# Hybrid attention and Mamba-2 step: last group split at column 272, work around it and at the start reordered

## The chip, the cores and the metric

The kernel runs on one core of one Trainium2 chip. The metric is the device time of one execution in microseconds; of several runs the median is taken. The core has five engines that this text names PE (matmuls), DVE (vector), ACT (activations), POOL (GpSimd) and SP (which only issues DMAs here).

## The reference, cut to what matters

Two layers are computed for 528 prompt tokens (16 meta tokens and 512 of the prompt) and 32 sample tokens, 560 columns in all. Layer 0 is windowed attention with sinks, layer 1 a Mamba-2 mixer. Everything is float32.

```python
hp = rmsnorm(xp, norm_w[i]); hs = rmsnorm(xs, norm_w[i])
# layer 0
q, k, v, g = split(u @ w_in); q, k = rmsnorm(q), rmsnorm(k)
out = (attend_with_sink(q, k, v) * silu(g)) @ w_out
# layer 1
z, xbc, dt = split(u @ w_in)
xs, B, C = split(silu(conv(xbc) + conv_b))
y = ssd_chunked(xs, dt, A, B, C, state) + d_skip * xs
y = y * silu(z)
y = y * rsqrt(mean over the group of y*y) * norm_w     # 4 groups of 512 channels
out = y @ w_out
xp = xp + out
```

## The kernel before, in words

Channels lie on the 128 partitions and tokens along the columns: `x` is 8 tiles of 128 x 560. Columns 0 to 15 are the meta tokens, then come four blocks of 128 prompt tokens (they begin at 16, 144, 272, 400) and from 528 on the 32 sample tokens. A float32 product is made of three fast matmuls: each operand is split into a rounded high part and a low remainder, and high x high, high x low and low x high are added (L1091 to L1093 in `project`).

**Weights.** `plan` lists the slabs (1 MB each: `kv`, `q`, `gate`, `out` of the attention stages, `dt`, `bc`, `x`, `z`, `out` of the Mamba stages) and the order of the half tiles that PE projects. SP loads a slab into one of two raw buffers, ACT rounds it (L644, `split_hi`), POOL subtracts to get the low half (L580, `split_lo`) into one of two buffers. POOL waits there until the slab two before has been used. A slab is loaded when the raw buffer is free of both.

**Order.** The order on each engine is written out by hand; a semaphore count for each product (`p_done`) and each evacuation (`p_evac`) ties them together. PE may start a half tile once the one two before has been evacuated (two PSUM banks).

**Start.** SP loads the prompt in four parts, then slabs. ACT issues the identity, meta tokens, sample tokens and six small parameter loads. PE transposes the parameters (L1141, L1142), then `x` tile by tile (L1154); ACT copies each tile out (L699) and squares rows for the norm (L693); DVE splits each tile into high and low (L1543, L1544, `split_x`). `first_tile` multiplies the first key tile as the splits appear, sums the squares (L1105) and adds the low weights (L1133).

**Between the layers.** `out` of the last attention stage is projected in 16 half tiles, and behind each finished tile DVE adds it into `x` (L1562) and splits it for layer 1 (L1543, L1544); ACT squares it (L670), POOL and DVE add up the squares, PE sums them (`sum_x`, L1113) after the `dt` projection.

**Mamba groups.** For each group g of 4, six units are run (`ORDER`: the samples, the meta block, the four prompt blocks). `start_states` on PE treats the 8 sample states in four pairs and fills with `z` half tiles (`fill_pairs`); DVE updates the states (L2023). Then for unit u: `prepare` and `new_state`, `mix` (L1862), `z` evacuation (L2007), `add_skip` of the unit before (L1896 to L1899) on DVE; `part_a`, `part_b` and a `z` half tile on PE; the decays (L971, L973) on ACT; the decay differences (L618) and the state's decay (L593) on POOL. After the last unit: SiLU of `z` (L1018), `gate_y` (L1907), squares (L1022), `sum_y` (L1408), scale (L1028, L1029), `norm_y` (L1914), high part (L927), `low_y` (L1922), each for two parts of the columns, 16 to 399 and 400 to 559. In groups 0 to 2 this is spread over the next group's convolution. In the last group it stands alone, followed by the output projection and the transposes of the result (L1519, L1520).

## Time and profile before

| | us |
|---|---|
| median of 3 runs (1063.0 to 1065.41) | 1065.17 |
| the profiled execution | 1069.09 |
| its span | 1067.0 |
| PE busy | 998.2 |
| DVE busy | 608.0 |
| ACT busy | 455.2 |
| POOL busy | 364.3 |

The span runs from the first to the last instruction; the execution's own time has 2.1 us around it. PE is busy for 94% of the span, so what can be gained lies in its waits, in the start and end where it does little, and in nothing that only another engine does beside it.

### The profile page before, as it was taken

To read this page: it belongs to the slowest core of one execution; us is meant where nothing else is said; L and a number is where in the kernel's file an instruction comes from. 1 tells how busy PE (TensorE), PEld (TensorE's weight loads), DVE (VectorE), ACT (ScalarE), POOL (GpSimd) and SP (SyncE) were. 2 spreads that over 40 slices of the span, in tenths; PEclk is the share of its full clock that TensorE was granted. 3 is DMA by queue.
4 is the path that set the end of the run, shared out by engine and by line. 5 is a ranking of instruction groups with operands and counts; after the bars stand their busy time and mean duration, and the time that the engine had idled before them with its cause. 6 is when DMAs were issued, how large, how long until landed. Compare 5 with 4: busy or idle time off the path is not lost.

```text
span 1067.0 us, 18613 instructions
## 1 busy us (share of the span) xinstructions
PE 998.2 (94%) x7408; PEld 918.3 (86%) x7408; DVE 608.0 (57%) x1449; ACT 455.2 (43%) x800; POOL 364.3 (34%) x275
## 2 busy tenths in 40 slices
PE   5999999999999899998897899999999999999978
PEld 4998899979998699977896778998899987997868
DVE  4215431363225242256888477976879767896872
ACT  4324623355134533346333445533463436526262
POOL 1531133113331132212724053642344343542520
PEclk9999999999999999999998899999999999999989
DMA  6432122232222222200233552327342372426302
GB/s 190 144 103 91 48 80 72 70 141 75 65 86 97 83 76 85 81 21 1 79 102 102 142 169 73 129 64 202 115 145 86 94 208 65 135 72 186 109 16 85
DMA packets 144118, 106.37 MB, mean 100 GB/s; under 512 B 10258, under 2 KB 135364, under 8 KB 143840
## 3 DMA queue, kind: packets, MB, share of 16 engines
q1 hardware_dynamic: 117160, 92.12, 27.7%
q10 hardware_dynamic: 26872, 13.06, 4.6%
q8 instruction: 59, 0.97, 0.4%
q14 instruction: 27, 0.22, 0.1%
HBM read 92.44 MB, written 16.79 MB: 102 GB/s over the span
## 4 chain that ended last, share of the span: by engine, by line
PE 71%; DVE 15%; issue 5%; ACT 3%; DMA 3%; SPq 1%; POOL 1%; ACTq 1%; DVEq 0%; POOLq 0%
PE pp L1091 18%; PE pp L1093 17%; PE pp L1092 17%; DVE cv L1773 2%; DMA w_raw_buf<-in_w_attn_out 2%; PE pS L1187 1%; PE pO L1402 1%; PE pO L1398 1%; PE pT_ L1388 1%; PE pO L1162 1%; PE pS L1408 1%; DVE z L1914 1%; DVE s_in L2023 1%; PE pO L1349 1%; SPq L463 1%
## 5 line engine op out<-in xcount | busy, mean ns | idle before, releaser
L580 POOL TENSOR_TENSOR w_lo_buf<-w_raw_buf,w_hi_buf 128x512 fp32r<-128x512 f32 x226 | 304.9, 1381 | 560.4 <-ACT w_hi_buf L644 457.3
L1091 PE MATMUL pp<-h_hi,w_hi_buf 128*128 128x280 f32 (+1 forms) x1264 | 386.6, 306 | 5.5 <-DVE rb L1747 3.8
L1093 PE MATMUL pp<-h_hi,w_lo_buf 128*128 128x280 f32 (+1 forms) x1264 | 370.0, 293 | 0.0
L1092 PE MATMUL pp<-h_lo,w_hi_buf 128*128 128x280 f32 (+1 forms) x1264 | 369.6, 292 | 0.0
L1091 PEld LDWEIGHTS pp<-h_hi,w_hi_buf 128*128 128x128 f32 x1264 | 240.7, 190 | 16.9 <-issue 8.2
L1092 PEld LDWEIGHTS pp<-h_lo,w_hi_buf 128*128 128x128 f32 x1264 | 240.7, 190 | 5.0 <-issue 4.6
L1093 PEld LDWEIGHTS pp<-h_hi,w_lo_buf 128*128 128x128 f32 x1264 | 240.7, 190 | 0.0
L644 ACT ACTIVATE w_hi_buf<-w_raw_buf 128x2048 fp32r<-128x2048 f32 (+1 forms) x57 | 107.8, 1892 | 22.1 <-DMA w_raw_buf<-in_w_ssm_in 11.5
L1562 DVE TENSOR_TENSOR x<-x,pp 128x272 f32<-128x272 f32 (+2 forms) x128 | 56.2, 440 | 84.8 <-PE pp L1093 84.0
L1091 PE MATMUL pp<-og_hi,w_hi_buf 128*128 128x280 f32 (+2 forms) x256 | 76.5, 299 | 5.6 <-DVE x L1562 4.4
L1091 PE MATMUL pp<-y_hi,w_hi_buf 128*128 128x272 f32 x256 | 76.6, 299 | 1.8 <-DVE y_lo L1922 0.8
L1093 PE MATMUL pp<-og_hi,w_lo_buf 128*128 128x280 f32 (+2 forms) x256 | 75.2, 294 | 0.0
L1092 PE MATMUL pp<-og_lo,w_hi_buf 128*128 128x280 f32 (+2 forms) x256 | 75.0, 293 | 0.0
L1093 PE MATMUL pp<-y_hi,w_lo_buf 128*128 128x272 f32 x256 | 74.5, 291 | 0.0
L1092 PE MATMUL pp<-y_lo,w_hi_buf 128*128 128x272 f32 x256 | 74.2, 290 | 0.0
L1773 DVE SCALAR_TENSOR_TENSOR cv<-rb,par,cv 128x584 f32<-128x584 f32 x69 | 69.5, 1007 | 1.1
L1556 DVE TENSOR_TENSOR q<-pp,rs 128x280 f32<-128x280 f32 x32 | 14.4, 449 | 84.2 <-PE pp L1093 84.2
L1091 PEld LDWEIGHTS pp<-og_hi,w_hi_buf 128*128 128x128 f32 x256 | 48.8, 190 | 7.5 <-DVE x L1562 4.1
L971 ACT ACTIVATE seg<-seg 128x1024 f32<-128x1024 f32 (+1 forms) x20 | 18.7, 933 | 85.7 <-issue 44.6
L1091 PEld LDWEIGHTS pp<-y_hi,w_hi_buf 128*128 128x128 f32 x256 | 48.8, 191 | 4.1 <-DVE x L1562 2.3
L728 ACT ACTIVATE sm<-sm,nm,crow 128x256 f32<-128x256 f32 (+2 forms) x80 | 42.3, 531 | 19.7 <-DVE ds L1600 19.7
L1092 PEld LDWEIGHTS pp<-og_lo,w_hi_buf 128*128 128x128 f32 x256 | 48.9, 191 | 0.2 <-issue 0.2
(304 smaller groups left out, 1651.1 us busy)
## 6 DMA issues: line engine op xcount, KB each, us to landing
w_raw_buf<-in_w_attn_in SPq DMA_DIRECT2D x16, 1024.0 KB, 5.2
w_raw_buf<-in_w_ssm_in SPq DMA_DIRECT2D x16, 1024.0 KB, 5.5
w_raw_buf<-in_w_attn_out SPq DMA_DIRECT2D x8, 1024.0 KB, 6.9
s_in<-in_state_ssm SPq DMA_DIRECT2D x32, 256.0 KB, 4.2
out<-s_in SPq DMA_DIRECT2D x32, 256.0 KB, 3.2
seg<-a_scratch ACTq DMA_DIRECT2D x16, 512.0 KB, 4.4
w_raw_buf<-in_w_ssm_out SPq DMA_DIRECT2D x8, 1024.0 KB, 5.2
w_raw_buf<-in_w_attn_in SPq DMA_DIRECT2D x8, 512.0 KB, 6.1
```

The source lines that it names most:

```text
L463: sp.dma_start(dtb[:, :], dt_bias.rearrange("a h -> h a"), allow_slow_non_contiguous=True).then_inc(s_late, 16)
L580: ins = pool.tensor_tensor(w_lo_buf[n % LO_SLOTS][:, piece], raw[n % RAW_SLOTS][:, piece], w_hi_buf[n % HI_SLOTS][:, piece].bitcast(F32), ...
L644: act.activation(w_hi_buf[n % HI_SLOTS][:, 0:m], raw[n % RAW_SLOTS][:, 0:m], ACT.Copy).then_inc(w_hi, 1)
L728: act.activation(p, p, ACT.Exp, bias=nm[0:n, v % 2, h:h + 1], scale=crow[0:n, cc + h:cc + h + 1], accum_out=den[0:n, v % 2, h:h + 1])
L971: act.activation(e, e, ACT.Relu, scale=-1.0).then_inc(clamped, 1)
L1091: pe.matmul(dst, hi[:, k, cols], a_hi[:, k, tk], start=(k == 0), stop=False)
L1092: pe.matmul(dst, hi[:, k, cols], a_lo[:, k, tk], start=False, stop=False)
L1093: mm = pe.matmul(dst, lo[:, k, cols], a_hi[:, k, tk], start=False, stop=(k == depth - 1))
L1162: pe.matmul(misc[:, colsum(c) + h:colsum(c) + h + 1], src[:, COL[c]:COL[c] + P], ones[:, 0:1], start=True, stop=True)
L1556: dve.tensor_tensor(dst[:, tk], bank(kind, s, tile, half), rs[:, tk], ALU.mult).then_inc(p_evac, 1)
L1562: dve.tensor_tensor(x[:, tile, tk], x[:, tile, tk], bank("out", s, tile, half), ALU.add).then_inc(p_evac, 1)
L1773: ins = dve.scalar_tensor_tensor(w[:, 0:CONV_OUT], r[:, tap:tap + CONV_OUT], conv_wc(tap, ct), w[:, 0:CONV_OUT], ALU.mult, ALU.add)
```

## The change

Four places are changed, not only the one of the title.

At the start, PE first runs 20 matmuls on a tile of ones. The sample tokens are loaded first on SP's queue, the two norm weights ahead of the other parameters on ACT's; meta and sample tokens share a row block. DVE waits for the norm weights alone. ACT rounds the first slab in two column halves ahead of the squares, POOL makes its low half in two parts, and the first tile takes the low weights in from k = 5 on. The second key/value tile goes to a free PSUM bank; the sum of the squares comes after its first half. In every attention stage the key transposes come ahead of the sum of key squares.

Between the layers, ACT makes the high part of `x` (one activation with a scale), and DVE only the low part, on a schedule (`low_after`).

In the last group, the parts are columns 16 to 271 and 272 to 559, for `z`, for the gate and norm and for the output projection. The four `z` half tiles of the first part come first, one more of them inside `start_states`, none in the last unit. The first part's SiLU is done in unit 2, its gate ahead of unit 5's `new_state` and `mix`, its norm and low part ahead of the last `add_skip`; the second part's steps and the last `new_state` stand between the first output half tiles. The last two slabs' low halves are written over the raw slab, without waiting for a low buffer, and the last is made before unit 5's state decay.

```diff
+WARM = 20
+LOW_FROM = 5
@@ def span(kind, stage, half):
+    if (kind, stage) == ("out", STAGES - 1):
+        return slice(COL[3], T) if half else slice(N_META, COL[3])
+def z_order(stage):
+    if stage == STAGES - 1:
+        return [(t, half) for half in range(2) for t in range(4)]
+    return [(t, half) for t in range(4) for half in range(2)]
@@ fill_pairs
-            return (0, 1, 2) if g + 1 < GROUPS else (0,)
+            return (0, 1, 2) if g + 1 < GROUPS else (0, 1)
@@ part_of
+            edge = EARLY if g + 1 < GROUPS else COL[3]
+            return slice(edge, T) if part else slice(N_META, edge)
+        def low_buf(n):
+            in_place = n >= len(slabs) - RAW_SLOTS
+            return w_lo_raw[n % RAW_SLOTS][:, :] if in_place else w_lo_buf[n % LO_SLOTS][:, :]
@@ sync
+            sp.dma_start(xtok[0:32, 4, :], x_sample.rearrange("b s d -> (b s) d")).then_inc(s_xs, 16)
@@ gpsimd
-                    if n >= LO_SLOTS:
+                    if n >= LO_SLOTS and n < len(slabs) - RAW_SLOTS:
                         pool.wait_ge(p_done, slab_done(n - LO_SLOTS))
+            for i, (rounded, ready) in enumerate(((first_hi, first_lo), (w_hi, w_lo))):
...
+                if i:
+                    pool.wait_ge(h_ready, KM - 2)
...
+                if g + 1 == GROUPS:
+                    split_lo(len(slabs))
                 decay_state(g, UNITS - 1)
@@ scalar
             def square_x(k):
-                act.wait_ge(h_ready, KM + k + 1)
+                act.wait_ge(p_evac, tile_done("out", GROUPS - 1, k))
+                act.activation(h_hi[:, k, :], x[:, k, :], ACT.Copy, scale=norm_c(1, k)).then_inc(high_x, 1)
...
+            for k in range(KM):
+                copy_x(k)
+                if k == 0:
+                    act.wait_ge(par_tr, 1)
+                    act.activation(par[:, 122:154], misc[:, 128:160], ACT.Copy).then_inc(par_ready, 1)
+                if k == 4:
+                    round_first(0)
                 if k == 6:
+                    round_first(1)
...
+            for m in range(len(SQUARED)):
+                square_tokens(m)
+                if m == 2:
                     split_hi()
...
+                    if (g, u) == (GROUPS - 1, 2):
+                        silu_z(z_order(s)[0:HEADS])
+                        exp_tables()
...
+                if g + 1 == GROUPS:
+                    high_y(g, 0)
+                    silu_z(z_order(s)[HEADS:])
@@ tensor
+            for i in range(WARM):
+                pe.matmul(pp[:, i % 2, 0:P], ones[:, :], ones[:, :], start=True, stop=True)
...
+                else:
+                    sum_y(g, 0)
+                    part_b(g, UNITS - 1)
...
             for n, (t, half) in enumerate(out_order(STAGES - 1)):
                 project("out", STAGES - 1, t, half)
-                if n == 0:
+                if n == 4:
+                    sum_y(GROUPS - 1, 1)
+                if n == 8:
                     final_state(GROUPS - 1)
@@ vector
+            low_after = [()] * 5 + [(0,), (), (1,), (2,), (3,), (), (4,), (), (5,), (6,), (7,)]
...
                 add_out(GROUPS - 1, t, (half,))
-                if half:
-                    dve.wait_ge(p_evac, tile_done("out", GROUPS - 1, t))
-                    split_x(1, t)
+                for k in low_after[n]:
+                    dve.wait_ge(high_x, k + 1)
+                    dve.scalar_tensor_tensor(h_lo[:, k, :], x[:, k, :], norm_c(1, k), h_hi[:, k, :].bitcast(F32),
...
                     prepare(g, u)
+                    if (g, u) == (GROUPS - 1, UNITS - 1):
+                        gate_y(g, 0)
                     new_state(g, u - 1)
...
+            norm_y(GROUPS - 1, 0)
+            low_y(GROUPS - 1, 0)
+            add_skip(GROUPS - 1, UNITS - 1)
+            for n, (t, half) in enumerate(out_order(STAGES - 1)):
                 add_out(STAGES - 1, t, (half,))
+                if n < 2:
+                    gate_y(GROUPS - 1, 1, (2 * n, 2 * n + 1))
+                if n == 2:
+                    new_state(GROUPS - 1, UNITS - 1)
+                if n == 4:
+                    norm_y(GROUPS - 1, 1)
+                if n in (5, 6):
+                    low_y(GROUPS - 1, 1, (2 * n - 10, 2 * n - 9))
```

## Rows read from the trace of the kernel before

**Rows 1.** The page, busy time of each engine.
```profile
PE 998.2 (94%) x7408; PEld 918.3 (86%) x7408; DVE 608.0 (57%) x1449; ACT 455.2 (43%) x800; POOL 364.3 (34%) x275
```
**Rows 2.** The cores, with span and mean granted TensorE clock.
```profile
core 0: 1067.0 us, clock 0.984
```
**Rows 3.** Waits from 484 to 532: waiter <- releaser: us in total, times, longest.
```profile
ACT sqx L670 <- DVE h_lo L1544: 17.8, 8, 3.3
...
PE pp L1091 <- DVE x L1562: 4.4, 5, 1.4
```
**Rows 4.** Timeline, PE, start: start us, us, what, count [idle before <- releaser].
```profile
10.11 0.44 PE L1141 MATMUL pO<-cst,partok 122*128 122x122 f32 x1 [10.11 <-DMA partok<-in_ssm_norm_w]
...
10.61 1.55 PE L1154 MATMUL pS<-cst,xtok 16*128 16x16 f32 x6
...
30.35 1.61 PE L1105 MATMUL pO<-cst,ssum 128*128 128x128 f32 x12
...
42.39 0.37 PE L1091 MATMUL pp<-h_hi,w_hi_buf 128*128 128x280 f32 x1 [0.18 <-issue]
```
**Rows 5.** The transposes of x: DMAs of its source from issue to landing.
```profile
DMA to landing us min/median/max: 4.1/6.0/8.1
```
**Rows 6.** Timeline, DVE, start.
```profile
12.94 0.51 DVE L1543 TENSOR_SCALAR h_hi<-x,par 128x560 fp32r<-128x560 f32 x1 [12.94 <-ACT x L699]
13.49 0.80 DVE L1544 SCALAR_TENSOR_TENSOR h_lo<-x,par,h_hi 128x560 fp32r<-128x560 f32 x1
...
25.96 1.70 DVE L1544 SCALAR_TENSOR_TENSOR h_lo<-x,par,h_hi 128x560 fp32r<-128x560 f32 x1
```
**Rows 7.** Timeline, POOL: low halves at the start, between the layers, at the end.
```profile
24.34 5.71 POOL L580 TENSOR_TENSOR w_lo_buf<-w_raw_buf,w_hi_buf 128x512 fp32r<-128x512 f32 x4 [23.08 <-ACT w_hi_buf L644]
...
499.71 5.93 POOL L580 TENSOR_TENSOR w_lo_buf<-w_raw_buf,w_hi_buf 128x512 fp32r<-128x512 f32 x4 [31.59 <-ACT w_hi_buf L644]
...
1023.11 5.47 POOL L580 TENSOR_TENSOR w_lo_buf<-w_raw_buf,w_hi_buf 128x512 fp32r<-128x512 f32 x4
```
**Rows 8.** Timeline, PE, between the layers.
```profile
503.48 0.40 PE L1091 MATMUL pp<-og_hi,w_hi_buf 128*128 128x288 f32 x1 [0.28 <-DVE x L1562]
...
522.94 0.29 PE L1091 MATMUL pS<-h_hi,w_hi_buf 128*128 128x280 f32 x1
...
526.64 0.40 PE L1091 MATMUL pS<-h_hi,w_hi_buf 128*128 128x280 f32 x1 [0.85 <-DVE h_lo L1544]
```
**Rows 9.** Timeline, DVE, start states of group 2 (851 to 858) and group 3.
```profile
851.56 2.15 DVE L2023 SCALAR_TENSOR_TENSOR s_in<-s_in,dec_s,pS 128x128 f32<-128x128 f32 x8 [0.67 <-PE pS L1359]
...
857.09 2.16 DVE L2023 SCALAR_TENSOR_TENSOR s_in<-s_in,dec_s,pS 128x128 f32<-128x128 f32 x8 [1.81 <-PE pS L1359]
...
975.66 2.15 DVE L2023 SCALAR_TENSOR_TENSOR s_in<-s_in,dec_s,pS 128x128 f32<-128x128 f32 x8 [0.67 <-PE pS L1359]
...
978.47 1.64 DVE L2023 SCALAR_TENSOR_TENSOR s_in<-s_in,dec_s,pS 128x128 f32<-128x128 f32 x6 [0.65 <-PE pS L1359]
```
**Rows 10.** Timeline, DVE, last unit and norm of group 3, one output half tile.
```profile
1016.04 1.23 DVE L1862 TENSOR_TENSOR seg<-seg,cbm 128x1024 f32<-128x1024 f32 x1 [1.38 <-ACT seg L973]
...
1019.69 1.96 DVE L1907 TENSOR_TENSOR z<-z,y 128x384 f32<-128x384 f32 x4
...
1026.19 3.04 DVE L1907 TENSOR_TENSOR z<-z,y 128x160 f32<-128x160 f32 x4
1029.16 2.19 DVE L1914 SCALAR_TENSOR_TENSOR z<-z,par,rg 128x384 f32<-128x384 f32 x4
...
1038.73 0.44 DVE L1562 TENSOR_TENSOR x<-x,pp 128x272 f32<-128x272 f32 x1 [1.07 <-PE pp L1093]
```
**Rows 11.** Timeline, PE, first output matmul.
```profile
1031.96 0.57 PE L1091 MATMUL pp<-y_hi,w_hi_buf 128*128 128x272 f32 x1 [0.81 <-DVE y_lo L1922]
```
**Rows 12.** Timeline, ACT, group 3.
```profile
996.16 1.06 ACT L971 ACTIVATE seg<-seg 128x1024 f32<-128x1024 f32 x1 [5.98 <-POOL seg L618]
...
1016.95 1.28 ACT L1018 ACT_TABLE_LOAD   x1
```

More of the change, by code:

```diff
@@ L123, in add @@
             slabs.append((kind, stage, i))
-            if kind == "out" and stage >= GROUPS - 1:
+            if kind == "out" and stage >= GROUPS - 1 or kind == "z":
                 continue
@@ L130, in add @@
             halves.extend((kind, stage, t, half) for t, half in out_order(stage))
+        if kind == "z":
+            halves.extend((kind, stage, t, half) for t, half in z_order(stage))
     for s in range(GROUPS):
@@ L225, in build @@
         w_lo_buf = [at(f"w_lo{i}_buf", [P, W_SLAB], F32R) for i in range(LO_SLOTS)]
+        w_lo_raw = [at(f"w_lo_raw{i}", [P, W_SLAB], F32R, offset=where[f"w_raw{i}_buf"]) for i in range(RAW_SLOTS)]
         par = at("par", [P, 154])
@@ L263, in build @@
         end1 = top[0]
-        xtok = at("xtok", [P, 6, D_MODEL], offset=where["gate"])
+        xtok = at("xtok", [P, 5, D_MODEL], offset=where["gate"])
         tsq = [at(f"tsq{i}", [P, D_MODEL], offset=where["q"] + 4 * D_MODEL * i) for i in range(2)]
@@ L926, in high_y @@
                     act.wait_ge(yn_ready, 8 * g + 4 * part + t + 1)
-                    act.activation(y_hi[:, t, part_of(part)], z[:, t, part_of(part)], ACT.Copy).then_inc(og_hi, 1)
+                    tk = part_of(g, part)
+                    act.activation(y_hi[:, t, tk], z[:, t, tk], ACT.Copy).then_inc(og_hi, 1)
             for g in range(GROUPS):
@@ L1003, in _, with silu_z @@
                 act.activation(sT[1][:, :], pT_[:, 1, :], ACT.Copy).then_inc(yo_copied, 1)
+                def silu_z(parts):
+                    for t, half in parts:
+                        act.wait_ge(p_evac, half_no[("z", s, t, half)] + 1)
+                        act.activation(z[:, t, span("z", s, half)], z[:, t, span("z", s, half)],
+                                       ACT.Silu).then_inc(silu_ready, 1)
                 for u in range(2, UNITS):
@@ L1081, in project @@
                     a_hi, a_lo = h_hi, h_lo
-                dst = (pS[:, half, :] if kind == "dt" else pp[:, j % 2, :])[:, 0:tk.stop - tk.start]
+                spare = kind == "dt" or (kind, s, tile) == ("kv", 0, 1)
+                dst = (pS[:, half, :] if spare else pp[:, j % 2, :])[:, 0:tk.stop - tk.start]
                 for k in range(depth):
@@ L1100, in sum_tokens @@
             def sum_tokens():
-                for c in SQUARE_ORDER:
-                    n = LEN[c]
-                    pe.wait_ge(tsq_ready, SQUARE_ORDER.index(c) + 1)
-                    mm = pe.matmul(fO[:, X_AT + COL[c]:X_AT + COL[c] + n], ssum[0:n, c:c + 1].to_broadcast([n, P]),
-                                   ident[0:n, 0:n], start=True, stop=True)
+                pe.wait_ge(tsq_ready, len(SQUARED))
+                for c in range(6):
+                    rows = slice(ROW_AT[c][1], ROW_AT[c][1] + LEN[c])
+                    col = c % 5
+                    mm = pe.matmul(fO[:, X_AT + COL[c]:X_AT + COL[c] + LEN[c]],
+                                   ssum[rows, col:col + 1].to_broadcast([LEN[c], P]), ident[rows, rows],
+                                   start=True, stop=True)
                 mm.then_inc(ssx_done, 1)
@@ L1242, in _ @@
                         tile_of("out", s - 1, t)
-                pe.wait_ge(ksq_ready, s + 1)
-                if s:
-                    pe.wait_ge(soft_a, UNITS * s)
-                else:
-                    pe.wait_ge(x_ready, KM)
-                for half in range(2):
-                    mm = pe.matmul(pS[:, half, 0:HALF], ones[:, :], ksq[:, half * HALF:(half + 1) * HALF],
-                                   start=True, stop=True)
-                mm.then_inc(kss_done, 1)
                 pe.wait_ge(kc_in, 16 * (s + 1))
@@ L1259, in _ @@
                 mm.then_inc(kct_tr, 1)
+                pe.wait_ge(ksq_ready, s + 1)
+                if s:
+                    pe.wait_ge(soft_a, UNITS * s)
+                else:
+                    pe.wait_ge(p_evac, tile_done("kv", 0, 1))
+                for half in range(2):
+                    mm = pe.matmul(pS[:, half, 0:HALF], ones[:, :], ksq[:, half * HALF:(half + 1) * HALF],
+                                   start=True, stop=True)
+                mm.then_inc(kss_done, 1)
                 tile_of("q", s, 0)
@@ L1473, in _ @@
                         project("out", s - 1, t, half)
-                part = [(t, half) for t in range(4) for half in range(2)]
+                part = z_order(s)
                 project("z", s, *part.pop(0))
@@ L1549, in bank @@
                 dve.wait_ge(p_done, j + 1)
-                return (pS[:, half, :] if kind == "dt" else pp[:, j % 2, :])[:, 0:tk.stop - tk.start]
+                spare = kind == "dt" or (kind, s, tile) == ("kv", 0, 1)
+                return (pS[:, half, :] if spare else pp[:, j % 2, :])[:, 0:tk.stop - tk.start]
             def scaled(dst, kind, s, tile, parts=(0, 1)):
@@ L2001, in _ @@
                     conv_last(g)
-                part = [(t, half) for t in range(4) for half in range(2)]
+                part = z_order(s)
                 def evac_z():
```

199 lines of the change are left out of this document (115 added, 84 removed).

## The prediction

> **What bounds the kernel now.** I read the page first: PE is busy 94% of the span [rows 1], at a mean granted clock of 0.984 [rows 2]. PE's work stays nearly the same, so the change can only shorten its waits. Then I read the timeline of PE with the idle time ahead of each piece, and looked at what the other engines did there. Three stretches answer to the diff.
>
> The start: PE's first instruction waits 10.11 us for the last of the small parameter loads, then transposes, and the first `q` tile begins at 42.39 [rows 4]. Between the two the pace is DVE's, 0.51 and 0.80 us for each tile of `x`, begun at 12.94 [rows 6].
>
> Between the layers PE waits five times, 4.4 us, for DVE's addition into `x`, while ACT waits 17.8 us for DVE [rows 3]: DVE is the bound there and ACT is idle.
>
> The end: PE begins the last output projection at 1031.96 [rows 11]. DVE finished `mix` of the last unit at 1017.27 [rows 10]; the 14.7 us between are a chain of gate, square, sum, scale, norm and low part.
>
> **The start, step by step.** PE now needs the identity, the first quarter of the prompt, and meta and sample tokens. Those loads took 4.1 to 8.1 us, 6.0 in the middle [rows 5]. With their issue near 0.7 I take PE's first transpose at 6.5. From PE's start to DVE's took 12.94 - 10.61 = 2.33 us [rows 4, 6]; with the copy of the norm weights in between I put DVE's start at 9.2. If the loads come no sooner than before, it is 12.9; that is the other end. The 20 warm-up matmuls lie in PE's idle 10 us and cost nothing; without that cover they would stand ahead of the transposes.
>
> DVE's eight tiles take about 1.37 us each, 11.0 us. POOL now works beside them: four operations took 5.71 us [rows 7], and beside them DVE's 0.80 became 1.70 [rows 6]: twice as long. So half of 5.6 us is lost, 2.8. DVE ends at 9.2 + 11.0 + 2.8 = 23.0 and PE has the first tile at 23.4.
>
> A half tile of 12 matmuls of 272 columns takes 1.07 + 0.44 = 1.51 us [rows 10], so 24 of 280 take 3.1. Then: half of the second tile 3.1, the token sums 1.5 (1.61 with the tail, [rows 4]), the other half 3.1, key transposes and key sums about 1.0 each: `q` begins at 23.4 + 9.7 = 33.1 instead of 42.39, 9.3 us sooner. I take off 0.8 for ACT's squares, which now come behind all copies and may hold the token sums. **Gain 8.5, between 4.8** (loads no sooner) **and 10.5** (no loss beside POOL, squares in time). Moving the key transposes ahead of the key sums in the later stages costs and gains nothing: both stand in a row on a busy PE.
>
> What shows that rows 6 and 7 decide the size: by the Trainium skill, page "SBUF — State Buffer", section "Who interferes with whom", a DVE instruction with two SBUF inputs and a GpSimd instruction that reads SBUF exclude each other for the whole instruction, and the second one fully blocks. By that the loss could be all of 5.6 us here, and the gain 5.7. The trace shows about half (0.90 more on 0.80 us beside a POOL operation of 5.71 / 4 = 1.43), and I go by it.
>
> **Between the layers.** Nine half tiles are left at 503.2 and `dt` begins at 522.94 [rows 8]: 19.7 us. Undisturbed they take 4 x 1.51 and, at 288 columns, 5 x 1.60, together 14.0. DVE's load per tile falls by its first operation, and ACT takes that into its 17.8 us of waiting [rows 3]; eight activations on 560 columns fit in. That gives 5.7; the 0.85 wait of `dt` for the low part [rows 8] makes it 6.6. What comes next is the low half of the second slab, which POOL ended at 505.6 [rows 7] and which PE now wants at 504.8: 0.6 with what is around it. **Gain 6.0, between 1.5** (rival below) **and 7.** Behind it DVE's convolution chain starts from the sum of squares, which PE issues after `dt`, so it moves with PE.
>
> **The last group.** First a cost. A fourth `z` half tile goes into `start_states`, in pair 1. Group 2 has it there: its state updates of pair 1 and pair 2 stand 857.09 - 851.56 = 5.53 us apart, in group 3 without it 978.47 - 975.66 = 2.81 [rows 9]. So all that follows is **2.7 us later**; leaving out `z` in the last unit gives next to nothing back, since DVE and not PE paces the units.
>
> The early SiLU fits into ACT's 5.98 us wait for POOL: two table loads of 1.28 and four half-width activations [rows 12]. DVE is free for `mix` at 1016.04 - 1.38 = 1014.66 [rows 10]; now at 1017.4. The first gate comes in: four of 384 columns took 1.96 alone, four of 160 beside POOL 3.04 [rows 10]. Since the last low half is made then (5.47 us [rows 7], moved ahead of the state decay), I take 2.6 for 256 columns: 1020.0. `mix` beside POOL 1.7: 1021.7. From the end of `mix` to the first gate stood 2.4 us, with a `z` evacuation of 0.44 that now falls away [rows 10], so `add_skip` is 2.0: 1023.7. By then ACT's squares, PE's sum and the scale are through. From the start of `norm_y` to the first output matmul took 1031.96 - 1029.16 = 2.8 us at 384 columns [rows 10, 11]; at 256 I take 2.4. PE starts at **1026.2, 5.8 us sooner**.
>
> Then DVE has ahead of it 8 additions of 0.44, `add_skip` 2.0, and at 288 columns three quarters of the rows for 384: gates 1.5, norms 1.6, low parts about the same, and some 0.7 for `new_state`: 11 us, and a wait for the second scale. PE's sixteen half tiles cost what they did, eight at 1.43 (256 columns) and eight at 1.60 (288) for sixteen at 1.51. Out of the stage goes the slow start of the first one (its first matmul shows 0.57 [rows 11]; 1.3 us for the tile), since PE is now kept busy by the sum and `part_b` ahead of it; in come the second sum, 1.2, and some 1.7 of waits for DVE, whose 11 us and the wait for the scale just fill the first eight half tiles and the sum, 12.6. So the rest is 1.6 us longer than before, and 5.8 becomes 4.2. `new_state` and the state's DMA end well ahead of the last result. **Gain 4.2, between 1** (DVE's work holds PE up for 5) **and 7** (no loss beside POOL, second norm hidden). The wait for the second `z` slab's low half, wanted earlier now, is covered.
>
> **The sum.** 8.5 + 6.0 + 4.2 = 18.7 us. The profiled execution took 1069.09 and the changed one would take 1050.4. The median of the runs shown is 1065.17, 3.9 lower, so I predict 1065.2 - 18.7, **1046.5 us**. A measurement of this kernel can tell about 0.3%, 3.2 us, from no change.
>
> **Rivals.**
> - Loads no sooner. The start's order changes, but DVE still begins near 12.9. For it: the queue is full of 512 KB loads. Against: 6.0 us in the middle [rows 5] and the wait of 10.11 for the small loads alone. Gain 15.0: 1050.2.
> - DVE stands still for the whole of each POOL operation beside it: 2.8 more at the start and about 1.5 in the last group. Gain 14.4: 1050.8. For it: the doubled 0.80 [rows 6]; against: it was doubled and not more. It is the rule that the Trainium skill states in the place named above.
> - ACT becomes the bound between the layers: the high part of tile k + 2 stands behind a square that waits for POOL's sum, and POOL is in a low half of 5.93 us [rows 7]. Then `dt` waits for `h_lo` instead. Gain there 1.5, in all 14.2: 1051.0.
> - The last group gives nothing: the 2.7 of the extra `z` and the full DVE between output tiles eat the head start. For it: 11 us of DVE's work against 12.6 of PE's; against: most of it was DVE's before too. Gain 14.5: 1050.7.
> - On the other side: TensorE's granted clock falls. PE's waits are also its rests; with less of them the 998 us busy [rows 1] would run at a lower mean than 0.984 [rows 2]. Each hundredth costs 10 us. It decides from 0.965 on, where the gain is gone, and below 0.962 the kernel is slower, by over 3.2 us: 1069 or more. Against it: the mean is that near to one although PE is already busy for 94% of the time.
>
> **How the numbers follow.** Chances: forecast 0.72, loads no sooner 0.07, blocked in full 0.07, ACT the bound 0.05, last group nothing 0.07, clock 0.02. All but the clock stay at 1051 alone; two together reach 1055. The bounds of the three gains, 7.3 and 24.5 if all were met at once, are reached only in part: about two thirds of the way from the forecast to either gives 1042.5 and 1054. The upper side is where most of the rivals lie and the lower one where only unhidden losses fall away; the range is 1041 to 1053. Faster by over 0.3%: 0.96; within: 0.02; slower: 0.02.
>
> **What would show it.** In the profile after: PE's first transpose near 6.5 and DVE's first split near 9; `q` at 33 to 34; no waits of PE for DVE's additions between the layers and `dt` about 14 us after the same point; state updates of group 3 5.5 us apart in pair 1; the first output matmul some 5.8 us nearer to the start of the group than before. Wrong would be: DVE's first split at 13, a wait of PE on the token sums of over 1 us, `dt` waiting for `h_lo` at each k, or an output stage of over 39 us (35.0 from 1031.96 to the span's end before).

## The result and the profile after

| | before | after |
|---|---|---|
| median of the timed runs, us | 1064.09 (1062.44 to 1065.41, 4 runs) | 1052.13 (1051.42 to 1052.82, 4 runs) |
| the profiled execution, us | 1069.09 | 1051.91 |

The ratio is 0.9888, interval 0.9870 to 0.9907: 1.1% faster, 12.0 us by the medians. Forecast were 18.7 us of gain and 1046.5 us, range 1041 to 1053. The sign and the range held, the range by 0.9 us. The forecast time was 5.6 us too low; the gain fell short by 6.7, the other 1.1 being the median of the kernel before, which is lower with its fourth run. One timed run of experiment 2 below took 1371.19 us at a granted clock of 0.652, and it is left out of that experiment's median.

The page of the changed kernel, busy time of each engine (beside [rows 1]):

```profile
PE 997.0 (95%) x7448; PEld 916.8 (87%) x7448; DVE 603.0 (57%) x1441; ACT 462.4 (44%) x813; POOL 366.5 (35%) x275
```

Its cores (beside [rows 2]):

```profile
core 0: 1050.1 us, clock 0.985
```

PE's busy time and mean clock stayed, so the gain is waits removed, as supposed. To place it I compare when PE reaches the same point of the program. The second profile of the kernel before is from a run told of below.

| PE begins | before | before, again | after | lead of after, us |
|---|---|---|---|---|
| first `q` tile | 42.39 | 42.03 | 35.83 | 6.6 / 6.2 |
| last eight transposes of the attention | 486.43 | 483.98 | 478.88 | 7.6 / 5.1 |
| `dt` | 522.94 | 518.99 | 511.53 | 11.4 / 7.5 |
| states of group 3 | 970.74 | 967.05 | 956.50 | 14.2 / 10.6 |
| first matmul of the last output projection | 1031.96 | 1027.26 | 1013.71 | 18.3 / 13.6 |
| span's end | 1067.0 | 1062.6 | 1050.1 | 16.9 / 12.5 |

The first profile of before exaggerates the gain by 4.4 us, the distance of the two columns of lead at the end; the second one agrees with the medians.

**Start.** The changed kernel's timeline, PE (beside [rows 4]; start, duration, what, idle time before it):

```profile
1.06 7.39 PE L1226 MATMUL pp<-ones 128*128 128x128 f32 x40 [1.06 <-POOL eps L596]
8.38 0.99 PE L1239 MATMUL pS<-cst,xtok 16*128 16x16 f32 x6
...
25.23 0.40 PE L1211 MATMUL pp<-h_hi,w_hi_buf 128*128 128x280 f32 x1 [2.15 <-DVE h_lo L1643]
...
35.83 0.50 PE L1174 MATMUL pp<-h_hi,w_hi_buf 128*128 128x280 f32 x1
```

Its DVE (beside [rows 6]):

```profile
10.23 0.51 DVE L1642 TENSOR_SCALAR h_hi<-x,par 128x560 fp32r<-128x560 f32 x1 [10.23 <-ACT par L753]
10.78 0.80 DVE L1643 SCALAR_TENSOR_TENSOR h_lo<-x,par,h_hi 128x560 fp32r<-128x560 f32 x1
...
15.27 1.53 DVE L1642 TENSOR_SCALAR h_hi<-x,par 128x560 fp32r<-128x560 f32 x1
16.84 1.72 DVE L1643 SCALAR_TENSOR_TENSOR h_lo<-x,par,h_hi 128x560 fp32r<-128x560 f32 x1
...
23.49 1.68 DVE L1643 SCALAR_TENSOR_TENSOR h_lo<-x,par,h_hi 128x560 fp32r<-128x560 f32 x1
```

Two things to see. The transposes begin right behind the warm-up matmuls: PE waited for nothing there but its own queue. And DVE's operations grow by 0.9 to 1.0 us wherever POOL is at a low half.

**Between the layers.** The waits of 476 to 525 (beside [rows 3]):

```profile
PE pp L1174 <- DVE x L1662: 1.4, 2, 0.9
ACT sqx L714 <- POOL xsum L643: 1.2, 1, 1.2
```

ACT's 17.8 us of waiting for DVE are gone, and of PE's five waits two are left, 0.56 and 0.86. The second one has a chain behind it, in ACT, DVE and PE:

```profile
504.52 1.92 ACT L687 ACTIVATE w_hi_buf<-w_raw_buf 128x2048 fp32r<-128x2048 f32 x1 [3.55 <-DMA w_raw_buf<-in_w_ssm_in]
...
507.12 0.80 DVE L1797 SCALAR_TENSOR_TENSOR h_lo<-x,par,h_hi 128x560 fp32r<-128x560 f32 x1 [2.41 <-ACT h_hi L711]
...
508.32 0.39 PE L1174 MATMUL pp<-og_hi,w_hi_buf 128*128 128x272 f32 x1 [0.86 <-DVE x L1662]
```

ACT waits for a slab to land and rounds it before it makes the next high part of `x`; DVE waits for that high part ahead of its next addition, and PE for the addition.

**Last group.** DVE in the states (beside [rows 9]):

```profile
961.40 2.16 DVE L2127 SCALAR_TENSOR_TENSOR s_in<-s_in,dec_s,pS 128x128 f32<-128x128 f32 x8 [0.67 <-PE pS L1454]
964.66 0.44 DVE L2111 TENSOR_TENSOR z<-pp,rs 128x272 f32<-128x272 f32 x1 [1.10 <-PE pp L1176]
966.92 2.15 DVE L2127 SCALAR_TENSOR_TENSOR s_in<-s_in,dec_s,pS 128x128 f32<-128x128 f32 x8 [1.81 <-PE pS L1454]
968.99 0.41 DVE L1965 TENSOR_TENSOR seg<-seg,cbm 32x256 f32<-32x256 f32 x1
```

DVE and POOL in the last unit (beside [rows 7, 10]):

```profile
1001.57 5.71 DVE L2011 TENSOR_TENSOR z<-z,y 128x256 f32<-128x256 f32 x4
...
1001.06 5.95 POOL L610 TENSOR_TENSOR w_lo_raw<-w_raw_buf,w_hi_buf 128x512 fp32r<-128x512 f32 x4
```

PE there (beside [rows 11]):

```profile
1004.14 2.05 PE L1504 MATMUL pS<-xc,ones 128*128 128x256 f32 x4 [4.16 <-ACT xc L1094]
...
1013.71 0.68 PE L1174 MATMUL pp<-y_hi,w_hi_buf 128*128 128x256 f32 x1
```

The update of pair 1 stands 5.52 us ahead of pair 2's, as in group 2 before. The four first gates took 5.7 us, about as long as POOL's four operations. PE waited 4.16 us for the first square, and the granted clock was 0.50 from 1004 to 1010, that is 1.2 GHz. The wait is not the gates' doing, as experiments 2 and 5 show.

### The profile page after: what moved, and what is told of

It is laid out like the page before. It is cut to its first block, busy times and chain, and to the rows that moved or that the text cites. A ratio compares the mean times of both kernels' runs of the same rounds, so it can differ in the third digit from the quotient of the medians.

```text
span 1050.1 us, 18698 instructions
## 1 busy us (share of the span) xinstructions
PE 997.0 (95%) x7448; PEld 916.8 (87%) x7448; DVE 603.0 (57%) x1441; ACT 462.4 (44%) x813; POOL 366.5 (35%) x275
## 4 chain that ended last, share of the span: by engine, by line
PE 73%; DVE 14%; issue 4%; ACT 3%; DMA 3%; SPq 2%; POOL 1%; DVEq 0%; ACTq 0%; POOLq 0%
PE pp L1174 18%; PE pp L1176 17%; PE pp L1175 17%; DVE cv L1876 2%; DMA w_raw_buf<-in_w_attn_out 2%; PE pO L1493 2%; PE pO L1497 2%; PE pT_ L1483 2%; PE pS L1278 1%; PE pS L1504 1%; PE pO L1253 1%; SPq L493 1%; DVE s_in L2127 1%; PE pO L1444 1%; PE pS L1416 1%
## 5 line engine op out<-in xcount | busy, mean ns | idle before, releaser
L610 POOL TENSOR_TENSOR w_lo_buf<-w_raw_buf,w_hi_buf 128x512 fp32r<-128x512 f32 x214 | 289.2, 1382 | 525.3 <-ACT w_hi_buf L687 433.7
L1174 PE MATMUL pp<-h_hi,w_hi_buf 128*128 128x280 f32 (+1 forms) x1248 | 381.0, 305 | 5.1 <-DVE rb L1850 4.6
L1176 PE MATMUL pp<-h_hi,w_lo_buf 128*128 128x280 f32 (+1 forms) x1248 | 363.9, 292 | 0.0
L1175 PE MATMUL pp<-h_lo,w_hi_buf 128*128 128x280 f32 (+1 forms) x1248 | 363.5, 291 | 0.0
L1174 PEld LDWEIGHTS pp<-h_hi,w_hi_buf 128*128 128x128 f32 x1248 | 236.5, 189 | 16.7 <-issue 8.3
L1176 PEld LDWEIGHTS pp<-h_hi,w_lo_buf 128*128 128x128 f32 x1248 | 236.3, 189 | 0.0
L1662 DVE TENSOR_TENSOR x<-x,pp 128x272 f32<-128x272 f32 (+3 forms) x128 | 56.2, 440 | 80.8 <-PE pp L1176 80.0
L1174 PE MATMUL pp<-y_hi,w_hi_buf 128*128 128x272 f32 (+2 forms) x256 | 76.6, 299 | 1.7 <-DVE x L1662 1.6
L1175 PE MATMUL pp<-y_lo,w_hi_buf 128*128 128x272 f32 (+2 forms) x256 | 73.7, 288 | 0.0
L1176 PE MATMUL pp<-y_hi,w_lo_buf 128*128 128x272 f32 x192 | 55.4, 289 | 0.0
```

Of the source, the lines that this page charges most:

```text
L610: ins = pool.tensor_tensor(low_buf(n)[:, piece], raw[n % RAW_SLOTS][:, piece], w_hi_buf[n % HI_SLOTS][:, piece].bitcast(F32), ALU.subtract)
L1174: pe.matmul(dst, hi[:, k, cols], a_hi[:, k, tk], start=(k == 0), stop=False)
L1175: pe.matmul(dst, hi[:, k, cols], a_lo[:, k, tk], start=False, stop=False)
L1176: mm = pe.matmul(dst, lo[:, k, cols], a_hi[:, k, tk], start=False, stop=(k == depth - 1))
L1662: dve.tensor_tensor(x[:, tile, tk], x[:, tile, tk], bank("out", s, tile, half), ALU.add).then_inc(p_evac, 1)
```

## The experiments

All kernels are timed against the kernel before on the same chip. An interval of 0.2 to 0.3% is 2 to 3 us, so for effects of 1 us the profile's points of the program decide; "lead" is meant against the changed kernel at such a point.

**1. No warm-up.**

```
-WARM = 20
+WARM = 0
```

> The changed kernel without its 20 warm-up matmuls. In its profile they ran from 1.06 to 8.45 and the first transpose began at 8.38. Theory A (they stand ahead of the transposes and cost): the first transpose begins near 6.5, when the loads have landed, DVE's first split near 8.5 in place of 10.23, and the first q tile 1 to 1.9 us sooner than 35.83; in all 1 to 2 us faster than the changed kernel (1052.1). Theory B (the loads land only near 8.4 anyway): nothing moves, 0 within 0.3. Theory C (they pay by TensorE's clock): the transposes take 2 us and more per tile of x in place of 0.9, the granted clock at the start is lower, and the q tile comes as late as before or later, by 0 to 2 us.

Measured: 1050.62 us (ratio 0.9867, interval 0.9839 to 0.9894). Its PE:

```profile
5.37 1.54 PE L1239 MATMUL pS<-cst,xtok 16*128 16x16 f32 x6 [5.37 <-DMA xtok<-in_x_prompt]
7.25 0.31 PE L1243 MATMUL pO<-cst,partok 32*128 32x32 f32 x1 [0.34 <-DMA partok<-in_ssm_norm_w]
7.25 1.59 PE L1239 MATMUL pT_<-cst,xtok 16*128 16x16 f32 x6
```

The loads had landed at 5.37, 3 us before the changed kernel used them: theory A. But a tile of `x` then takes 1.29 us (7.25 to 8.54) in place of 0.89, which is theory C. The view of windows gives a granted clock of 1.00 for 6 to 12 here, so that row does not say why the transposes are slower, and the lower granted clock that theory C expected is not seen. DVE ended 2.8 us sooner, at 22.39, and `q` began at 34.84, 1.0 sooner. Both hold, A is larger.

**2. The last low half behind the first part's low halves.** Ahead of it on POOL:

```
+                    pool.wait_ge(og_lo, 4 * (GROUPS + 1) + 8 * g + HEADS)
                     split_lo(len(slabs))
```

> The low half of the last weight slab waits until DVE has made the first part's low halves. Theory A (the POOL operation blocks DVE's four first gates, 5.7 us in place of the 1.4 that four operations of 256 columns take alone): the gates take 1.4 to 1.8 us, PE's wait of 4.16 for the first square falls to under 1.5, and the first output matmul comes 57.2 - 3.5 = about 53.7 us after the state update at the group's start; 2 to 3.5 us faster than the changed kernel, since DVE has some 2 us to spare in the first half of the output stage and the blocked operations there (two of the second gates) fit in. Rival (the gates are slow for another reason, for example ACT's squares on the same buffers): they still take 4 us and more, and nothing is gained. Rival 2 (given back later): the first output matmul is 3.5 us sooner, but PE then waits for the slab's low half at the fifth half tile or for the second norm, and the end moves by under 1 us.

Measured: 1051.57 us (0.9875, interval 0.9849 to 0.9900). Its DVE and POOL:

```profile
1000.57 1.42 DVE L2012 TENSOR_TENSOR z<-z,y 128x256 f32<-128x256 f32 x4
...
1013.78 2.65 DVE L2012 TENSOR_TENSOR z<-z,y 128x288 f32<-128x288 f32 x2
...
1010.44 5.68 POOL L610 TENSOR_TENSOR w_lo_raw<-w_raw_buf,w_hi_buf 128x512 fp32r<-128x512 f32 x4 [10.34 <-DVE y_lo L2027]
```

Its PE in the output stage:

```profile
1013.92 0.39 PE L1175 MATMUL pp<-y_hi,w_hi_buf 128*128 128x256 f32 x1 [1.33 <-DVE x L1663]
...
1016.82 0.39 PE L1175 MATMUL pp<-y_hi,w_hi_buf 128*128 128x256 f32 x1 [1.22 <-DVE x L1663]
```

The gates fell from 5.7 to 1.42 us, so POOL was their whole delay, and the output stage began 3.2 us nearer to the group's start. But PE's wait for the first square, expected under 1.5 us, was still 3.89: ACT begins that square right behind the last unit's decays, 46.3 us after the group's first state update here and 46.6 in the changed kernel. What the slow gates held up were the other three squares and DVE's own chain: the norm began 51.3 us after that update in place of 53.9. Then two second gates took 2.65 (0.82 in the changed kernel), PE waited for the additions behind them, and 3.0 us were lost again. Theory A on the gates' cause, rival 2 on the end: my guess that DVE had 2 us to spare there was wrong.

**3. The fourth `z` half tile out of pair 1.**

```
-            return (0, 1, 2) if g + 1 < GROUPS else (0, 1)
+            return (0, 1, 2) if g + 1 < GROUPS else (0,)
```

> The fourth z half tile goes from the states' pair 1 back to the end, as in the kernel before. Theory A (it costs 2.7 us in pair 1 and saves next to nothing in the last unit, since DVE paces the units): pair 1's state updates stand 2.8 us apart in place of 5.5, everything up to the last unit comes 2.7 us sooner, and of that 1.5 to 2.7 us stays at the end. Rival (PE's z work is 1.5 us wherever it stands, and the unit that takes the eighth half tile back, with a DVE evacuation of 0.44 ahead of add_skip and a PE tile ahead of the sum, gets longer by what pair 1 gets shorter): end within 0.7 us of the changed kernel.

Measured: 1051.78 us (0.9861, interval 0.9834 to 0.9889). Its DVE:

```profile
963.03 2.15 DVE L2127 SCALAR_TENSOR_TENSOR s_in<-s_in,dec_s,pS 128x128 f32<-128x128 f32 x8 [0.67 <-PE pS L1454]
965.84 2.16 DVE L2127 SCALAR_TENSOR_TENSOR s_in<-s_in,dec_s,pS 128x128 f32<-128x128 f32 x8 [0.66 <-PE pS L1454]
967.91 1.32 DVE L1965 TENSOR_TENSOR seg<-seg,cbm 32x256 f32<-32x256 f32 x1
```

Its POOL, beside that last line:

```profile
967.06 1.90 POOL L659 TENSOR_TENSOR seg<-seg,tok 128x1024 f32<-128x1024 f32 x1 [12.11 <-DMA seg<-a_scratch]
```

The spacing is 2.81 again. Behind the states the lead grew by 2.0 us, not 2.7: the `mix` of the first unit now lies beside POOL's subtraction and takes 1.32 in place of 0.41. At the end 1.1 was left. Neither side fits: theory A's lower end was 1.5, the rival's upper one 0.7.

**4. High part of `x` by DVE again, between the layers.** In the addition's loop:

```
+                    link(dve.tensor_scalar(h_hi[:, k, :], x[:, k, :], norm_c(1, k), None, ALU.mult))
                     dve.scalar_tensor_tensor(h_lo[:, k, :], ...
```

> Between the layers only: the high part of x is made by DVE again, right behind each tile's addition, as in the kernel before. Theory A (DVE's load per tile was the bound there): PE waits again five times for the addition into x, some 4 us in place of 1.4, dt begins 4 to 5.5 us later against the first output tile of the attention, and the kernel is 3.5 to 5.5 us slower than the changed one. Rival (the stretch was shortened by its later start against POOL's low halves, not by the move to ACT): under 1.5 us slower.

Measured: 1056.58 us (0.9910, interval 0.9888 to 0.9933). Its waits from 476 to 522:

```profile
ACT sqx L713 <- DVE h_lo L1796: 17.3, 8, 3.3
...
PE pp L1173 <- DVE x L1661: 4.4, 5, 1.4
```

Both old rows are back. From the values of the last attention unit to the sum of squares of `x` PE takes 37.0 us here and in both profiles of the kernel before, 32.0 to 32.4 in the changed kernel and five variants of it, and 30.9 to 31.2 in the three others (experiments 1, 6 and 9): 4.6 to 5.0 us, in three kernels 5.8 to 6.1. Theory A.

**5. The last low half behind the first gates alone.**

```
+                    pool.wait_ge(yz_ready, 8 * g + HEADS)
                     split_lo(len(slabs))
```

> The low half of the last slab waits for the four first gates alone. When it waited for the first part's low halves, the gates fell from 5.7 to 1.4 us and the first output matmul came 3.2 us sooner against the turn of y in the last group, but DVE then stood beside POOL in the output stage (the two pairs of second gates 2.65 and 1.33, add_skip's last addition 1.81), PE waited 1.33 and 1.22, and all was given back. Theory A (it is the place that counts: beside it should lie DVE work that reads PSUM or that waits anyway): now the low half lies beside mix, add_skip and a wait of DVE of 1.6 us for the scale; mix takes 2.6 in place of 1.2, the norm begins near 1 us later than there, the first output matmul comes 2 to 2.5 us sooner than in the changed kernel, the output stage takes as long as in the changed kernel (32.3 from its first matmul to the last), and the end comes 1.8 to 2.5 us sooner. Rival (the blocked time is lost wherever it lies): within 0.7 us of the changed kernel.

Measured: 1049.06 us (0.9851, interval 0.9830 to 0.9872). Its DVE, POOL and PE:

```profile
1000.50 1.42 DVE L2012 TENSOR_TENSOR z<-z,y 128x256 f32<-128x256 f32 x4
...
1002.43 1.92 DVE L1966 TENSOR_TENSOR seg<-seg,cbm 128x1024 f32<-128x1024 f32 x1
1004.27 0.68 DVE L2000 TENSOR_TENSOR ec<-ec,pO 128x512 f32<-128x512 f32 x1
1004.98 0.69 DVE L2002 TENSOR_TENSOR ec<-ec,pT_ 128x512 f32<-128x512 f32 x1
1005.71 1.55 DVE L2003 TENSOR_TENSOR y<-y,ec 128x512 f32<-128x512 f32 x1
1007.73 2.12 DVE L2019 SCALAR_TENSOR_TENSOR z<-z,par,rg_last 128x256 f32<-128x256 f32 x4 [0.47 <-ACT rg_last L1102]
...
1002.00 6.39 POOL L610 TENSOR_TENSOR w_lo_raw<-w_raw_buf,w_hi_buf 128x512 fp32r<-128x512 f32 x4 [1.97 <-DVE z L2012]
...
1002.98 3.75 PE L1505 MATMUL pS<-xc,ones 128*128 128x256 f32 x8 [4.08 <-ACT xc L1095]
```

Here the rule can be read off. The five DVE rows behind the gates all lie beside POOL's low half. The two that read `pO` or `pT_`, PSUM, keep their 0.68; the ones with both inputs in SBUF grow: 1.21 to 1.92, 0.69 to 1.55, and the four norms together, of which only the first lies beside POOL, from 1.67 to 2.12. What is lost lies in front of a wait for the scale, 1.58 us in experiment 2 and 0.47 here. PE begins the output stage 2.3 us sooner than in the changed kernel, and the end keeps 2.1 of it. Theory A. PE's wait for the first square is again about as long as with the slow gates, 4.08, and the granted clock behind it is low again, 0.59 from 1004.3 to 1010.3.

**6. Eleven warm-up matmuls.**

```
-WARM = 20
+WARM = 11
```

> Eleven warm-up matmuls in place of 20. With none the first transpose began at 5.37, when its loads had landed, but a tile of x took 1.29 us in place of 0.89, and of DVE's end 2.8 us sooner only 1.0 reached the q tile. Eleven at 0.37 us should end at 5.1. Theory A (the matmuls both stand in the way and pay by the rate): the first transpose begins at 5.2 to 5.5 and a tile takes 0.9 us, DVE begins at 7.8 and ends at 22.3, PE's first tile ends some 0.4 us behind it, and the q tile begins at 32.8 to 33.3 in place of 35.83: 2.5 to 3 us faster than the changed kernel. Rival (the rate comes back only after more of them, or is lost in the small wait for the norm weights): a tile takes 1.29 again, and q begins near 34.8.

Measured: 1050.13 us (0.9847, interval 0.9826 to 0.9868). Its PE:

```profile
1.06 4.65 PE L1226 MATMUL pp<-ones 128*128 128x128 f32 x22 [1.06 <-POOL eps L596]
5.64 0.99 PE L1239 MATMUL pS<-cst,xtok 16*128 16x16 f32 x6
7.74 0.24 PE L1243 MATMUL pO<-cst,partok 32*128 32x32 f32 x1 [1.11 <-DMA partok<-in_ssm_norm_w]
```

The transposes begin at 5.64 and keep the short duration (0.99 for six pieces, as in the changed kernel). `q` began at 34.01, 1.8 sooner, where 2.5 to 3 were expected: the norm weights landed at 7.7, so DVE began at 8.26, and beside POOL it ended at 23.34, not 22.3. Theory A by its mechanism, short by 0.7.

**7. The last group undone in full** (one edge for both parts, `z` in tile order, gate behind the last `mix`, sums, additions and low halves as in the kernel before).

> The last group is undone in full: one edge for both parts, z in its old order with three half tiles ahead, the gate of the last group behind the last mix, sums and low halves as in the kernel before. What it gives is then read against the changed kernel, without any difference of the start. Theory A (the trace's milestones tell it: the two kernels' group 3 and output stage differ by 2.6 us, 2.0 lost in pair 1 and 4.6 won behind it): state updates of pair 1 are 2.8 us apart, the end comes 2.2 to 3.0 us later than in the changed kernel. Rival (my own forecast of 4.2 holds and the profiled executions hid part of it): 3.5 to 4.5 us later. Rival 2 (some of it came from the head start of the first layer's end): under 1.5.

Measured: 1054.58 us (0.9895, interval 0.9879 to 0.9911). From the state update of group 3 to PE's last matmul it takes 1.7 us more than the changed kernel (2.0 less in pair 1, then 4.6 more up to the output stage, and 0.9 less in it). That is between theory A, whose lower end was 2.2, and rival 2. The first profile of before gave 2.6, the second one 1.9.

**8. The kernel before, again.**

> The kernel before once more, for a second profile. Its first profiled execution took 1069.09, 4 to 5 us over its median, and its span was 16.9 us longer than the changed kernel's, where the medians differ by 12. Theory A (single stretches take longer in some executions, where TensorE's granted clock falls behind a wait): this execution is some 3 to 5 us shorter, it agrees with the first to within 0.1 us up to the first such place, and the difference lies in one to four steps of 0.5 to 2 us behind waits of PE. Rival (it differs by a bit everywhere, in the transfers): no steps, but a drift.

Measured: 1064.68 us, one run. The lead over the first profile is 0.36 us from the first `q` tile to 362, 2.4 from 405 to 486, 3.6 to 4.2 from 495 to the last group and 4.4 at the end. These are steps: theory A. One of them, the same 12 us of the program in windows (duration, busy time and count of PE, PEld, DVE, ACT, POOL, granted clock, DMA share, GB/s), first profile:

```profile
483.00:495.00 12.00, 10.20 (x49) 7.72 (x49) 5.72 (x17) 8.46 (x22) 0.00 (x0) 0.86 0.01 1
```

Second profile:

```profile
481.00:493.00 12.00, 10.20 (x61) 7.73 (x60) 6.89 (x21) 9.29 (x24) 0.00 (x0) 1.00 0.01 1
```

PE is busy as long, does 61 instructions in place of 49, and the clock is 1.00 in place of 0.86: behind waits of 0.7 and 1.1 us it fell in one execution and not in the other. That is 1.5 us.

**9. Three edits together**: 11 warm-up matmuls, the low half behind the first gates, three `z` half tiles ahead.

> Three edits of the changed kernel at once: 11 warm-up matmuls, the last low half behind the first gates, three z half tiles ahead in the last group. In the profiles they gave 1.8, 2.2 and 1.1 us each. Theory A (they lie in different stretches and add up): the end comes some 5 us sooner than in the changed kernel's profile, about 1045 to 1047 in the timed runs, 1.018 to 1.022 faster than the kernel before. Rival (the eighth z half tile in the last unit takes what the gates gained, since DVE evacuates it ahead of add_skip and the norm): the z edit gives nothing here, 3.5 to 4 us in all.

Measured: 1048.50 us (1046.89 to 1049.40), ratio 0.9854, interval 0.9834 to 0.9875, against 1064.90. Its core:

```profile
core 0: 1045.1 us, clock 0.989
```

The span is 5.0 us shorter than the changed kernel's, but not by the three parts expected. At the first state product of group 3 the lead is 2.7 us, and from there to PE's last matmul it grows by 2.3, where experiment 5 alone gave 2.1 and experiment 3 alone 1.1. So the `z` edit gives 0.2 here, which is the rival's result. Its DVE, 49.2 us behind the group's first state update:

```profile
1003.59 3.46 DVE L2019 SCALAR_TENSOR_TENSOR z<-z,par,rg_last 128x256 f32<-128x256 f32 x4
```

With the eighth `z` half tile in the last unit PE waits only 1.04 us for the first square and the scale is there earlier, but the norm then meets POOL's low half and state decay: 3.46 us in place of 2.12 in experiment 5. PE begins the output stage 1.2 us sooner than there, but behind a wait of 3.21 us, and the granted clock is 0.72 in the stage's first 6 us (1.00 in experiment 5); 1.0 us is lost again.

The timed runs show less than the profile, 3.6 us between medians taken in different sessions, and a ratio that isn't better than that of experiment 5; 1045 to 1047 was expected and missed. It beats the kernel before by 1.3 to 1.7%; that it beats the changed kernel by 5 us is shown by one profile alone, of the fastest of its five runs.

**10. POOL behind the splits at the start.**

```
-LOW_FROM = 5
+LOW_FROM = 7
-                if i:
-                    pool.wait_ge(h_ready, KM - 2)
+                pool.wait_ge(h_ready, KM)
```

> At the start POOL makes the first slab's two low halves only when DVE has split all eight tiles of x, and PE takes the low part of the first tile at its end. In the changed kernel DVE's eight splits took 14.94 us where 8 x 1.26 = 10.1 stand without POOL. Theory A (the two engines shut each other out for whole operations): every split takes 1.26, DVE ends near 20.3 in place of 25.17, and the four POOL operations take 1.42 each from there; PE waits for them instead: they end near 26.0, the second weight tile begins there, and the q tile comes at 35.6 to 36.8, 0 to 1 us later than in the changed kernel. So what POOL cost DVE was not to be had by a delay alone. Rival (the splits are slow for another reason, for example ACT's copies and squares beside them): they stay near 1.87 on the mean and DVE ends after 24.

Measured: 1050.57 us (0.9870, interval 0.9849 to 0.9891). Its DVE, POOL and PE:

```profile
15.28 0.51 DVE L1641 TENSOR_SCALAR h_hi<-x,par 128x560 fp32r<-128x560 f32 x1
15.82 0.80 DVE L1642 SCALAR_TENSOR_TENSOR h_lo<-x,par,h_hi 128x560 fp32r<-128x560 f32 x1
...
18.34 0.80 DVE L1642 SCALAR_TENSOR_TENSOR h_lo<-x,par,h_hi 128x560 fp32r<-128x560 f32 x1
...
20.56 4.97 POOL L631 TENSOR_TENSOR w_lo_buf<-w_raw_buf,w_hi_buf 128x512 fp32r<-128x512 f32 x4 [19.31 <-DVE h_lo L1642]
...
23.12 3.61 PE L1217 MATMUL pp<-h_hi,w_lo_buf 128*128 128x280 f32 x16 [1.88 <-POOL w_lo_buf L631]
```

Each tile takes 1.26 us to the eighth, DVE ends at 20.40 in place of 25.17, with ACT's copies and squares as before. POOL's operation takes 1.24, where 1.42 was expected and the changed kernel has 1.6 (two in 3.26, two in 3.19). PE waits for POOL instead and `q` begins at 36.54: theory A. One thing besides the edit differs: behind PE's wait of 1.88 us the granted clock was 0.50 from 24 to 27, in the changed kernel 1.00 behind one of 2.15. POOL ended at 25.53 and PE's second tile began at 26.53, so by my estimate about 1.0 us of `q` is the clock. Without it `q` would come near 35.5, 0.3 sooner than in the changed kernel: of the 4.8 us that DVE lost hardly any was to be had by delaying POOL.

## Why the prediction was right in sign and range, and 5.6 us off

**Clock and baseline.** I set the sum against a profiled execution 3.9 us over the median and took the distance off at the end, which was right: the excess sits in steps, the one looked at closely being a stretch of low clock (experiment 8), and not in what the change touches. The rival of a falling clock did not come: 0.984 and 0.985. That the range held is in part luck: the working gives 1042.5 and 1054, the range stated is lower by 1 to 1.5 us without a reason, and all three gains erred to the same side.

**Start: 8.5 forecast, 6.2 to 6.6 measured.** Two steps failed, one was too short, and two erred on the safe side.
- "The 20 warm-up matmuls lie in PE's idle 10 us and cost nothing" is wrong. I priced the idle time of the kernel before, which the same change takes away. They took 7.39 us and set the transposes to 8.38 instead of 6.5; the loads were there at 5.4. DVE began at 10.23, not 9.2. Experiments 1 and 6 show 1.0 and 1.8 us for it. This was my own condition, "without that cover they would stand ahead of the transposes", and I didn't check it against the 6.5 that I gave a few lines up.
- "Half of 5.6 us is lost" beside POOL is wrong too. Eight splits took 14.94 us for 8 x 1.26 = 10.1: 4.9 us lost, in five DVE operations that grew by 0.9 to 1.0 us each. Four of them met the four POOL operations of the first slab, the fifth the first one of the second slab, begun at 23.11, which the forecast left out. So each POOL operation cost DVE one wait. It is less than the 1.4 us that the rival put on each, because POOL itself waits too: its operation takes 1.6 here and 1.24 alone (experiment 10). Experiments 5 and 10 show that it is the meeting that costs: without POOL beside them the same operations don't grow. The 1.70 for 0.80 [rows 6] reads as 0.90 of waiting for the rest of one POOL operation, and one instance can't show a share. The Trainium skill, page "SBUF — State Buffer", section "Who interferes with whom", has it as the runs show it: a DVE instruction with two SBUF inputs and a GpSimd instruction reading SBUF exclude each other, and the later one waits out the other. The page also names `tensor_scalar` as an operation that can, under conditions, take the ports that the two engines share; L1642 in this case, 1.53 in place of 0.51 beside POOL, agrees.
- PE had the first tile some 1.0 us behind DVE's end, forecast 0.4.
- On the safe side were the splits themselves, 10.1 us without POOL for the 11.0 forecast, and the 0.8 for ACT's squares: PE did not wait on the token sums.
- The tail agreed: 9.6 us from the first tile's end to `q`, forecast 9.7.

**Attention: 0 forecast.** -1.1 to +1.0 by the two profiles of before. From the first `q` tile to the last transposes the twelve traces take 442.0 to 444.3 us, and the kernel before alone has 442.0 and 444.0, so no effect of the moved key transposes can be told.

**Between the layers: 6.0 forecast, 4.6 to 5.0 measured**, 5.8 to 6.1 in three kernels. The mechanism is shown by experiment 4. The missing 1.1 is PE's wait for an addition at 508.32, 0.86 us here and 1.04 to 1.26 in the five variants that have it; in the three kernels it is absent. The traces show where it comes from, though no run tests it. The step that failed is "What comes next is the low half of the second slab", priced at 0.6: what came next was the load of a slab. SP issues it when POOL has finished with the raw buffer, at 497.78, and ACT rounds the slab ahead of the next high part of `x`. In the six kernels with PE's wait, ACT begins that rounding 6.8 to 7.2 us behind POOL's end and DVE waits 2.4 to 2.8 us for the high part; in the three without, it is 5.7 to 6.0 and 1.3 to 1.6. In experiment 1:

```profile
502.80 0.80 DVE L1797 SCALAR_TENSOR_TENSOR h_lo<-x,par,h_hi 128x560 fp32r<-128x560 f32 x1 [1.34 <-ACT h_hi L711]
```

Why the load lands a microsecond sooner in these three is open. The rival with ACT as the bound didn't come as described: one square waited 1.2 us for POOL's sum, and `dt` waited for nothing. But for this 1.1 ACT, behind the load, is the bound.

**From the sum of squares of `x` to group 3: 0 forecast.** The lead grows by 1.7 to 2.0 us; 1.3 of it is one stretch behind a wait of 3.1 us, in which the view of windows shows a granted clock of 0.72 after and 0.51 in both profiles of before. The wait is the same in all. Experiment 1, a variant of the changed kernel, shows 0.52 there and takes 441.2 us for the whole stretch, as the kernel before does (441.1 and 441.3); the changed kernel and the other variants take 439.3 to 440.3. So it isn't tied to what the change does there; what decides it is open.

**Last group: 4.2 forecast, 1.7 to 2.6 measured.**
- The fourth `z` half tile: 2.7 forecast by the spacing; 5.52 against 2.81 came as forecast, but PE was only 2.0 later, since `mix` behind it no longer met POOL (experiment 3).
- The gates: 2.6 forecast, 5.7 measured. This is the same mis-sized step as at the start. The rows chosen, 1.96 and 3.04 [rows 10], had POOL beside only part of the latter. Experiments 2 and 5 show 3.2 and 2.3 us of it at the output stage.
- "By then ACT's squares, PE's sum and the scale are through" left out a wait: PE stood 4.16 us ahead of the first square, with the clock at 1.2 GHz for the sums and `part_b` behind it. Faster gates leave it at 3.89 and 4.08 (experiments 2 and 5). It is filled where the eighth `z` half tile is in the last unit: 0.95 in experiment 3, 1.04 in experiment 9. So taking that half tile out, which was forecast to give "next to nothing back", opened a wait.
- So PE began the output stage 2.6 to 4.0 us sooner against the group's start, where 5.8 was forecast. The output stage then took 0.9 to 1.4 us longer, forecast 1.6.

The rival "blocked in full" had 0.07 and gave 1050.8. Its mechanism is what happened, together with the warm-up. Its price at the start, 5.6 in all, lay above the 4.9 lost. Its 1.5 in the last group was too low, since experiment 5 alone brought 2.1 back.

## What to carry to other kernels

A filler placed in idle time has to be priced against the idle time of the kernel with the change, not of the kernel before: what the change brings forward is what the filler then delays. Where GpSimd and VectorE run beside each other, look at which VectorE operands are in PSUM and put the GpSimd work beside those or beside a wait; moving it without such a place only moves the loss (experiments 2 and 10 against 5). Take a second profile of the baseline before comparing two traces: here 4.4 us of 16.9 were the baseline's own. And compare the granted clock of a stretch in both traces before a difference of 1 us is put down to an edit (experiment 10).

## What the runs showed of the hardware that was not expected

- TensorE's granted clock falls behind the same short waits in one execution and not in the next: 0.86 and 1.00 over the same 12 us, 1.5 us apart. From the first `q` tile to 362 the two profiles of the kernel before keep their distance to within 0.02 us, so single profiles can be compared step by step once these places are known.
- The start isn't as repeatable, and it is the clock again. In the changed kernel and the five others with the same start code (experiments 2, 3, 4, 5 and 7) PE waits 2.15 us for DVE's last low part. Behind it the granted clock stays 1.00 in three, with the first `q` tile at 35.74 to 35.83, and falls to 0.58 to 0.86 (24 to 27 and 27 to 30) in experiments 3, 5 and 7, with `q` at 36.35 to 36.89, although their transposes began 0.4 to 1.0 us sooner. Experiment 1 kept 1.00 there, so its 1.0 is a comparison at the same clock, of single executions.
- POOL's subtraction of 128x512 takes 1.24 us alone (experiment 10) and 1.43 to 1.63 beside DVE: it too waits, but less than the DVE operation of 0.5 or 0.8 us, which grows by 0.9 to 1.0.
